# Expert weight loads: one half of the second pair's first weights issued ahead of two waits, and the first pair's first releases and loads by quarters

## The reference, cut to what matters

```python
def expert_block(args):
    tok, e, g = args
    xb = h[tok]
    y = (jax.nn.silu(xb @ w1[e]) * (xb @ w3[e])) @ w2[e]
    return (y * g[:, None]).astype(h.dtype)
```

## Time and profile before

| what | value |
|---|---|
| runs | 1231.37, 1229.02, 1231.75 us; median 1231.37 |
| profiled execution, its own time | 1228.85 us |
| its span, first to last instruction | 1227.2 us |
| around the span (1228.85 - 1227.2) | 1.65 us |
| PE / PEld / DVE / ACT / POOL busy | 1188.8 / 816.1 / 673.6 / 503.5 / 53.6 us |
| bytes moved by DMA | 394.98 MB, mean 322 GB/s |
| mean granted TensorE clock | 0.999 of full speed |

### The profile page before, as it was taken

How to read it: one execution, slowest core, us unless ns; L and a number is a source line. 1 busy time by engine, 2 the same in 40 slices (tenths; PEclk the granted TensorE clock), 3 DMA queues, 4 the chain that set the end, 5 groups by cost and what they waited for, 6 DMA issues and landing times.

```text
span 1227.2 us, 16442 instructions
## 1 busy us (share of the span) xinstructions
PE 1188.8 (97%) x6522; PEld 816.1 (66%) x6522; DVE 673.6 (55%) x1206; ACT 503.5 (41%) x779; POOL 53.6 (4%) x103
## 2 busy tenths in 40 slices
PE   6999999999999999999999999999999999999997
PEld 2697688888889878888878786455444444544436
DVE  5689979887889787864476685112111111111126
ACT  1579563434565576344448384111111111111125
POOL 0100001000010000010001100000000000000000
PEclk9999999999999999999999999999999999999999
DMA  9996868888846555856567779999999999999991
GB/s 370 391 350 269 315 235 323 333 311 300 315 162 244 187 214 202 304 192 216 186 234 247 265 309 415 418 425 423 426 425 428 424 426 425 427 423 426 425 421 43
DMA packets 50987, 394.98 MB, mean 322 GB/s; under 512 B 6673, under 2 KB 8913, under 8 KB 11378
## 3 DMA queue, kind: packets, MB, share of 16 engines
q1 hardware_dynamic: 39618, 337.18, 68.6%
q0 software_dynamic: 9072, 53.92, 12.3%
q10 hardware_dynamic: 2240, 3.10, 0.9%
HBM read 390.68 MB, written 3.49 MB: 321 GB/s over the span
## 4 chain that ended last, share of the span: by engine, by line
PE 79%; DVE 8%; DMA 8%; ACT 3%; issue 1%; SPq 1%; DVEq 0%; ACTq 0%
PE psum L1400 16%; PE psum L770 10%; PE psum L773 10%; PE psum L777 10%; PE psum L1443 7%; DMA slabs<-in_w 5%; PE psum L1332 4%; PE psum L843 2%; PE psum L847 2%; PE psum L845 2%; DMA staged<-in_ada 2%; PE psum L1340 2%; DVE w_parts L2151 2%; PE psum L1095 1%; PE psum L1107 1%; PE psum L1086 1%
## 5 line engine op out<-in xcount | busy, mean ns | idle before, releaser
L2151 DVE TENSOR_TENSOR w_parts<-w_raw,w_parts 128x2048 fp32r<-128x2048 f32 x106 | 241.7, 2287 | 62.4 <-ACT w_parts L1533 62.3
L1533 ACT ACTIVATE w_parts<-w_raw 128x2048 fp32r<-128x2048 f32 x106 | 202.0, 1911 | 70.6 <-DMA w_raw<-in_units 70.5
L1400 PE MATMUL psum<-slabs,arena 128*64 128x512 f32 x768 | 223.2, 593 | 2.4 <-DMA w_odd_late<-in_w 1.8
L770 PE MATMUL psum<-w_parts,h_parts 128*128 128x512 f32 x392 | 155.2, 396 | 3.7 <-ACT h_parts L1533 1.9
L773 PE MATMUL psum<-w_parts,h_parts 128*128 128x512 f32 x392 | 153.0, 390 | 0.0
L1533 ACT ACTIVATE arena<-psum 128x512 f32<-128x512 f32 (+1 forms) x59 | 29.9, 509 | 295.3 <-PE psum L1419 141.7
L1400 PEld LDWEIGHTS psum<-slabs,arena 128*64 128x64 f32 x768 | 71.3, 137 | 112.7 <-issue 106.8
L777 PE MATMUL psum<-w_parts,h_parts 128*128 128x512 f32 x392 | 105.3, 390 | 0.6 <-DVE h_parts L2329 0.6
L2134 DVE CUSTOM_DVE_ANT_0 aring<-aring,cb 128x1024 f32<-128x1024 f32 x80 | 94.5, 1218 | 1.2 <-DMA aring<-in_ada 1.2
L770 PEld LDWEIGHTS psum<-w_parts,h_parts 128*128 128x128 f32 x392 | 73.6, 188 | 20.3 <-issue 2.9
L1400 PE MATMUL psum<-w_odd,arena 128*64 128x512 f32 x192 | 85.1, 593 | 0.4 <-DMA slabs<-in_w 0.4
(11 more groups left out here) (338 smaller groups left out, 1932.1 us busy)
## 6 DMA issues: line engine op xcount, KB each, us to landing
w_raw<-in_units SPq DMA_DIRECT2D x110, 1024.0 KB, 5.0
slabs<-in_w SPq DMA_DIRECT2D x52, 1024.0 KB, 15.4
slabs<-in_w SPq DMA_DIRECT2D x22, 2048.0 KB, 21.7
aring<-in_ada POOLq DMA_DIRECT2D x40, 1024.0 KB, 5.6
arena<-in_w SPq DMA_DIRECT2D x16, 2048.0 KB, 20.7
w_odd<-in_w SPq DMA_DIRECT2D x16, 2048.0 KB, 19.8
w_odd<-in_w SPq DMA_DIRECT2D x24, 1024.0 KB, 25.5
staged<-in_ada SPq DMA_DIRECT2D x8, 1024.0 KB, 18.7
```

What stands on the lines that cost most here:

```text
L770: mm(psum[:, bank, :], high(tile, tok), w_hi(k)[:, col:col + 512], start=first and bank not in begun, stop=False, skip_group_check=True)
L1400: ins = nc.tensor.matmul(psum[s * CAP:(s + 1) * CAP, w, :], xe_t[:, kt, s * CAP:(s + 1) * CAP], up_weights(w, s, b, kt), start=kt == 0, st ...
L1533: return nc.scalar.activation(out_ap, in_ap, func, **kw)
L2151: v.tensor_tensor(w_lo(k), raw(k), w_hi(k).bitcast(F32), ALU.subtract).then_inc(w_split, 1)
```

## The change

It does two things. First, SP issues `load_w1_odd(1, 1)` (the second half of w1 of expert 1 of the second pair, 1 MB to `w1_odd_late`) before its wait for unit `Z_AT + 6` (`unit_done` of `Z_AT + 7`) and before that of unit `WOUT_AT + 2`, and no longer behind both. Second, in the first pair PE raises `up1_half` also after kt == 1, and SP loads the first halves of the third pair's w1 as two quarters each, one quarter of both experts after each release. The counts of the later waits follow.

```diff
+            def load_w1_quarter(p, s, b, q, signal):
+                cols = slice(q * UNIT // 2, (q + 1) * UNIT // 2)
+                sp.dma_start(slab(0, s, b)[:, cols], a["w1"][p, s][:, cols]).then_inc(signal, 16)
+
...
             load_w3_half(1, 0, 1, 0)
+            load_w1_odd(1, 1)
             sp.wait_ge(unit_done, Z_AT + 7)
             load_w1_tile(0, 1, 0)
             load_unit(WOUT_AT + 2)
-            load_w1_odd(1, 1)
             load_unit(WOUT_AT + 3)
...
-            sp.wait_ge(up1_half, up1_half_from + 1)
-            for s in range(2):
-                load_w1_half(2, s, 0, 0, w1_begun)
+            for q in range(2):
+                sp.wait_ge(up1_half, up1_half_from + q + 1)
+                for s in range(2):
+                    load_w1_quarter(2, s, 0, q, w1_begun)
...
-                    sp.wait_ge(up1_half, up1_half_from + 2)
+                    sp.wait_ge(up1_half, up1_half_from + 3)
...
-                        if first and kt == 3:
+                        if first and (kt == 3 or kt == 1 and w == 0):
                             ins.then_inc(up1_half, 1)
...
-            pe.wait_ge(w1_begun, w1_begun_from + 32)
+            pe.wait_ge(w1_begun, w1_begun_from + 64)
```

## The result

| | before | changed |
|---|---|---|
| median of 18 runs each | 1230.28 us (1228.07 to 1235.43) | 1233.01 us (1230.54 to 1238.28) |
| the profiled execution | 1228.85, span 1227.2, clock 0.999 | 1235.8, span 1234.0, clock 0.996 |

The ratio is 1.0025, 95% interval 1.0015 to 1.0034: slower by 2.7 us. The forecast was no change (-0.1 us, chance of slower 0.08). Two later comparisons of the same pair gave 1.0024 [1.0008, 1.0039] and 1.0006 [0.9997, 1.0014]. All 43 runs of the changed kernel have a median of 1231.93, 144 runs of the kernel before 1230.28: +1.6 us. The direction is settled, the size is about 1 to 3 us (the third interval holds no change as well), and why it varies between comparisons is found only in part. The profiled execution of the changed kernel lies 2.8 us above its median: most of what follows between the two profiles is of that execution.

The account below looks back on a forecast made before the run. The prediction saw the expert stage as a nearly continuous DMA stream, with PE losing 3.8 us to late weights. Moved megabyte +0.3 us and quarters -0.4 summed to -0.1; forecast 1231.0 us, range 1228.8 to 1233.2.

Parts of the forecast that it names:

- part two: Early-released quarters in the first pair's pass: close the stream's gap at 762 to 764 us, net -0.4 us (-1.3 to 0).
- Lead gained at 765 us: 1.3 us: Stream behind the quarters: earlier release closes the 1.5 us gap, leaving it 1.3 us ahead (0.9 to 1.5).
- Left: -0.4 us: Quarters' net effect after lead is given back at 781.01 and 791.31 us: -0.4 us (-1.3 to 0).
- Part one, gain 0: Moved 1 MB load before the experts: only lengthens the idle stretch at 724 us, no later load starts earlier, gain 0.
- The unit's delay, 0.6 us (0.1 to 2.2): Unit WOUT_AT + 2, issued at 716.89: lands 0.6 us later because the moved megabyte runs ahead of its queue.
- the unit is late: Rival, backlog ahead of WOUT_AT + 2: up to 2.2 us delay, later loads into a shortened queue, +1.8 us, 1233.2; chance 0.10.
- I count half of it: Unit's 0.6 us delay at the end: half reaches it, +0.3 us (0 to +1.5), since PE has waits to give back.
- 3.8 us of waits: PE's total loss to late weights, near 926.66, at 1143.54 and in the last pair; the most the loads can give.
- 0 to 0.3 us, and take 0.1: Price of the two extra loads from cutting halves into quarters: 0 to 0.3 us, taken as 0.1.
- The give-back, 0.6 us at 781 and 0.3 at 791: Loads at 781.01 (w2) and 791.31 us meet a shorter queue: 0.6 and 0.3 us of the lead lost.
- After 800 us ... no gap can come back: Stream after 800 us: the queue grows by 2.5 us a pair, so no gap returns.
- the loads pay by number: Rival, quarters: each of two added loads costs 2.2 us, 4.4 less the gap's 1.5, +2.9 us, 1234.3; chance 0.03.

Follow-up runs that it names:

- e1: Only the moved megabyte, halves as before, against the kernel before: 1229.72 us against 1230.06, ratio 1.0000.
- e11: The changed kernel once more, for a third profile, against the kernel before: 1230.74 us, ratio 1.0006.
- e9: The kernel before with the gather of the first pair's second half done twice, PE 1.8 us late: 1231.05 us, ratio 1.0008.
- e2: Only the early release and the quarters, no moved megabyte, against the kernel before: 1231.65 us, ratio 1.0010.
- e8: Quarters and early release without the moved megabyte, plus the fourth pair's first w1 halves released after kt == 3, against the kernel before: 1229.15 us, ratio 0.9995.
- f4: Repeat of e2 (quarters and early release only), one execution: 1229.88 us against 1230.64 of the kernel before.
- f3: Repeat of the changed kernel, one execution, without the half-clock stretch: 1229.81 us against 1230.64 of the kernel before.
- e4: Early release without the moved megabyte, both experts' quarters joined in one 1 MB DMA, against the kernel before: 1230.98 us, ratio 1.0004.
- e12: Joined quarters as in e4, plus the fourth pair's first w1 halves released after kt == 3, against the kernel before: 1230.27 us, ratio 1.0008.
- e5: The changed kernel once more, on another chip, against the kernel before: 1232.03 us, ratio 1.0024.
- e3: Quarters without the moved megabyte, all four issued after kt == 3, no early release, against the kernel before: 1231.17 us, ratio 1.0014.
- f1: Repeat of e1 (only the moved megabyte), one execution: 1230.48 us against 1230.64 of the kernel before.
- e10: e2 (quarters only) with the same doubled gather as e9, making PE late, against the kernel before: 1234.63 us, ratio 1.0029.
- e6: The kernel before, unchanged, treated as a changed one: 1230.49 us, ratio 1.0003.
- e7: The kernel before plus the fourth pair's first w1 halves released after kt == 3 of the third pair's pass, no quarters: 1229.31 us, ratio 1.0000.
- f2: Second repeat of e1 (only the moved megabyte), one execution: 1229.99 us against 1230.64 of the kernel before.
- f5: The whole changed kernel plus the early release of e7, against the kernel before: 1230.14 us against 1230.57, ratio 0.9994.
- f6: e10 (quarters, PE late) plus the early release of e7, against the kernel before: 1230.98 us, ratio 1.0006.

## Why the prediction was wrong

The range held the time (1233.01 of 1228.8 to 1233.2); the sign did not come out as forecast. The step that failed is part two: "Lead gained at 765 us: 1.3 us", 0.9 of it given back, "Left: -0.4 us". In the four profiles of the changed kernel the quarters won -0.7 to +0.2 us against the two halves of before, and w2 behind them then lost 0.8 to 2.2 us where 0.6 was forecast. The sum also had no term for what the changed program pays at its end, 0.3 to 0.6 us at the output's last DMA and 0.15 outside the span. By its steps:

**Part one, gain 0: not contradicted.** e1 is 1.0000, within 1.7 us. The idle stretch at 724 us is longer, as forecast (0 GB/s from 724 to 729), and no later load starts earlier.

**The unit's delay, 0.6 us (0.1 to 2.2): at its lower bound.** It landed 4.87 us after issue (4.80 in e1, 5.04 in e11) against 4.68. With the move it took 4.77 to 5.04 us in eight profiles, without it 4.68 to 4.79 in twelve: the megabyte ahead was still moving, and that costs 0.1 us in the median, 0.3 at most. ACT's idle time before it shows it:

```profile
724.42 1.92 ACT L1538 ACTIVATE w_parts<-w_raw 128x2048 fp32r<-128x2048 f32 x1 [1.58 <-DMA w_raw<-in_units]
```

1.58 us, not 1.39. In the rival "the unit is late" the first half did not happen. Its second half did in the profile after, loads released late into a queue that the quarters had shortened, but there PE was late by the half clock.

**"I count half of it": wrong in the profiles.** It was argued that PE has 3.8 us of waits to give back and the stream sets the end. But where PE releases loads into a nearly dry queue, the stream moves with PE: e1's PE was 2.73 us late at 762 us and its stream 2.9 at the end, and e9 had 3.46 and 3.3. Of these, 1.1 and 1.7 us stem from ahead of 740 us and move everything; the 1.6 and 1.8 that came to PE between there and 762 show in the stream as 1.8 and 1.6. The waits of the last pair do not shrink, they travel; `w_odd_late` still costs 1.76 us in the changed kernel, 1.77 before:

```profile
1172.10 0.64 PE L1405 MATMUL psum<-slabs,arena 128*64 128x512 f32 x1 [1.76 <-DMA w_odd_late<-in_w]
```

The 3.8 us are no cushion against lateness at 760 us; they are what the stream lacks, whenever it starts. (The runs put e9's 1.8 us at 0.8 in the median, with an interval of -0.2 to +2.1, so the timed share is less sure than that of the profiles.)

**Part two, lead 1.3 us at 765: too large.** The early release does fill the queue where PE is on time, but the quarters are slower than their bytes. Against the 6.4 us of the two halves before, e2 won 1.0 us, e8 0.8, f4 0.7 and f3, the changed kernel with PE on time, 0.2; the joined loads of e4 and e12 won 1.1 and 1.4. In the profiled execution after, PE was late by the half clock: the quarters were issued 2.9 us before the load ahead landed, not 4.7, and took 6.5 us for 2 MB; in e5 and e11 it was 6.3 and 7.1. The price of the extra loads, "0 to 0.3 us, and take 0.1", was too low in a filled queue (0.5 to 1.3 us for the four, 0.1 to 0.4 for the joined two, over 4.9); in a short one nothing is seen (e3 against the halves).

**The give-back, 0.6 us at 781 and 0.3 at 791: too small.** The place was right and the size was not. Here are the w2 load at 781.01 and its counterparts; the loss is against 4.89 us in a full queue:

| profile | issued before the load ahead lands, us | lands after it, us |
|---|---|---|
| before | 4.7 | 4.89 |
| e3, quarters late | 4.8 | 5.21 |
| f3, changed | 4.3 | 5.72 |
| f4, quarters | 4.0 | 5.49 |
| f1, moved megabyte, no quarters | 3.7 | 5.11 |
| e2, quarters | 3.5 | 5.94 |
| e4, joined | 3.5 | 7.18 |
| e9, PE late, no quarters | 3.5 | 5.27 |
| e10, PE late, quarters | 3.1 | 6.04 |
| after, changed | 3.1 | 6.77 |
| e5, changed | 2.8 | 7.07 |

Four profiles without quarters that had 4.9 to 5.6 us in hand (e1, e6, e7, f2) landed at 4.88 to 4.89; e11, the changed kernel, at 5.78 with 3.5. The forecast interpolated one line, from 4.7 us in hand (no loss) to 3.0 (1.5 lost). The loss is 0.3 to 2.3 us with the quarters, more than without them at the same time in hand (0.2 and 0.4 us), and it comes after the lead was won, out of the same shortage: the quarters end the transfers of the block earlier while PE issues w2 when it did, so each microsecond of lead is a microsecond less in hand. A lead in a stream whose next load is released by PE was no lead here: e4, ahead by 1.1 us at 785, ended 0.6 behind PE. The forecast's bounds for what is left, -1.3 to 0, left out that the loss can exceed the gain. "After 800 us ... no gap can come back" failed too: in after, e5 and e10 a single load landing between 835 and 842 us took 1.1 to 1.6 us more than its bytes, with 10 to 13 us of queue ahead of it. All told, the stream ended 0 to 2.1 us behind PE's own lag in the nine profiles with quarters and no second early release, and -0.2 to 0.7 in the six without either.

That this is not the whole cost e3 shows: w2 was issued there as comfortably as before, and the time is 1.1 to 1.7 us longer all the same.

**No term for the clock.** Nothing in rows 6 showed a drop, and 6 of 20 profiles have one of 3.4 us near 755 us, with the change or without. It costs 1.6 us of PE. By itself that is in the spread of any kernel's runs. It may cost more with the quarters: of the changed kernel's 43 runs, the 17 with a mean clock of 0.998 or more have a median of 1230.74, the others 1233.01; of 126 runs of before these are 1229.41 and 1230.95. So the change costs 1.3 us where the mean clock stayed up and 2.1 where it was lower. The difference of 0.8 us is within the scatter of these runs, and a mean doesn't tell where the clock fell; that it explains why the parts (0 and +1.2 to +1.6) and the first comparison (+2.7) differ is not shown.

**The rival "the loads pay by number"** gave +2.9 us, near what was measured, for the wrong reason. The page "DMA: Bandwidth & Descriptors" of the Trainium skill, in "Rules for kernel authors", asks for at least 1 MiB per DMA, and its fit, made for DMAs issued from GpSimd, has some 2.0 us of fixed cost. Two added loads would pay 4.0 us by it; four quarters took 5.4 to 6.2 us in a filled queue (e2, e8, f4, f3), two of twice the size 5.3 and 5.0 (e4, e12). Measured and rule agree in the sign and not in the size: two added loads cost up to 1.2 us here, and w2 behind them and the end of the program the rest.

**What stays open.** Why w2 loses more behind the quarters than without them (7.2 us in e4, 5.3 in e9, with 3.5 us in hand in both); what made the steps near 835 us; why the output's last DMA takes half a microsecond longer in some of these programs; why e3 is as slow as e2 without the early release; and how much a late PE adds, which one profile each of e10 and e2 suggests.

## What to carry to other kernels

Count the lead of a stream at the first load that its consumer releases after the place you repair. If that load has too little queue in hand (here 0.2 to 2.3 us were lost at 2.8 to 4.3 us in hand, 0 to 0.3 at 4.7 and more), an earlier predecessor may only move the hole, and move it where it is larger. Look at the next hole too: with the same early release one pair later the loss was gone (e8, f5, f6), though no version beat the kernel before. By the profiles, price a delay of the releasing engine at full, not at half, where the queue runs nearly dry behind it. And compare the last DMAs of the two programs as well: a fixed cost there looks like a cost of the part that was changed.

## What the runs showed of the hardware

- When a queue that has run short is filled again, the DMA engines are busy at a low rate: 160 and 295 GB/s at a share of 0.90 and 1.03 (765 to 767 above), in the kernel before, with halves, 221 GB/s at 1.01, against 426 in a full stream.
- The same issue with the same queue ahead lands at very different times there: w2 5.3 to 7.2 us after its predecessor with 3.5 us in hand. In a full queue 2 MB take 4.89 us nearly every time, but a single load between 835 and 842 us took up to 1.6 us more (after, e5, e10).
- In a filled queue 2 MB took 5.0 and 5.3 us as two loads with rows of 4 KB, 5.4 to 6.2 us as four.
- Near 755 us the granted clock fell to 0.5, the level of 1.2 GHz, for 3.4 us in 6 of 20 profiles, each time right behind PE's pauses of 0.84 and 0.35 us before the first pair, which are the same length in the 14 others. It cost PE 1.6 us.
- The start of the program (before 57 us) varied from -0.1 to +8.3 us between executions, more than anything that the change does.
- The 1 MB unit WOUT_AT + 2 landed 4.68 to 4.79 us after issue where the load ahead of it was done or nearly so, and 4.77 to 5.04 us in the eight profiles with the moved megabyte.
- The same last output DMA from SP took 3.96 to 4.11 us in twelve profiles and 4.46 to 4.65 in eight, by program and not by execution.
